# A recurrence whose second head pair has its tokens on the other half of the partitions

## The reference

```python
def step(state, inp):
    r_t, w_t, k_t, v_t, kk_t, a_t = inp
    sa = jnp.einsum('bhvk,bhk->bhv', state, -kk_t)
    state = (state * w_t[:, :, None, :]
             + sa[..., None] * (kk_t * a_t)[:, :, None, :]
             + v_t[..., None] * k_t[:, :, None, :])
    return state, jnp.einsum('bhvk,bhk->bhv', state, r_t)
_, y = lax.scan(step, s0, (r, decay, k, v, kk, a))       # 1040 tokens, 16 heads
# then, for each head: y minus its mean over the head's 64 channels, over its deviation,
# times ln_w plus ln_b, plus a bonus, times a gate
```

## Time and profile before

| | |
|---|---|
| median of three runs | 2782.72 us |
| the profiled execution | 2786.39 us |
| its span, first to last instruction | 2784.5 us |
| PE busy, share of the span | 2571.4 us, 92% |
| weight loads (PEld) busy | 2141.3 us, 77% |
| DVE, ACT, POOL busy | 1561.2, 1315.8, 316.7 us |
| mean granted clock of PE | 0.973 |
| stretch of the recurrence in it | 1211 to 1767 us |

### The profile page before, as it was taken

The page is one execution under the profiler, slowest core; times in us unless marked ns, Lnnn a source line. Parts: engine busy times, 40 slices in busy tenths (PEclk is TensorE's granted clock), DMA queues, the critical chain, the costliest instruction groups (busy, mean ns, idle before and its releaser), DMA issues. The chain is left out here.

```text
span 2784.5 us, 65171 instructions
## 1 busy us (share of the span) xinstructions
PE 2571.4 (92%) x27593; PEld 2141.3 (77%) x27593; DVE 1561.2 (56%) x2370; ACT 1315.8 (47%) x2266; POOL 316.7 (11%) x367
## 2 busy tenths in 40 slices
PE   6999999999989999989999999899895999999992
PEld 6989896777766766679999889778784888888882
DVE  4566664443035555544444444553326888888884
ACT  5655542222134444334444444462223777777771
POOL 0121222332000000001212222100001000000002
PEclk9999999999999999999999999999996999999996
DMA  4443342222122323212222201244355999999976
GB/s 110 156 164 137 131 148 72 92 92 74 40 94 66 101 63 130 86 46 80 55 61 58 58 21 33 77 114 136 118 187 212 392 392 396 398 391 393 398 298 257
DMA packets 162645, 440.46 MB, mean 158 GB/s; under 512 B 16295, under 2 KB 96825, under 8 KB 150097
## 3 DMA queue, kind: packets, MB, share of 16 engines
q1 hardware_dynamic: 146413, 381.95, 38.5%
q10 hardware_dynamic: 9060, 29.56, 2.8%
q0 software_dynamic: 6912, 25.17, 2.4%
HBM read 344.22 MB, written 92.41 MB: 157 GB/s over the span
## 5 line engine op out<-in xcount | busy, mean ns | idle before, releaser
L2610 DVE TENSOR_TENSOR ex_wL<-wx,ex_wH 128x2048 fp32r<-128x2048 f32 x192 | 436.0, 2285 | 46.6 <-ACT ex_wH L2514 44.8
L2514 ACT CAST ex_wH<-wx 128x2048 fp32r<-128x2048 f32 x192 | 366.4, 1911 | 94.3 <-PE ex_bank L2410 70.9
L2408 PE MATMUL ex_bank<-ex_wH,ex_xTH 128*128 128x512 f32 x512 | 200.5, 392 | 2.4 <-DVE ex_xTL L2615 2.4
L2409 PE MATMUL ex_bank<-ex_wH,ex_xTL 128*128 128x512 f32 x512 | 200.1, 391 | 0.0
L2410 PE MATMUL ex_bank<-ex_wL,ex_xTH 128*128 128x512 f32 x512 | 200.1, 391 | 0.0
L709 PE MATMUL ph_acc<-ph_wH,uH 128*104 128x512 f32 x480 | 192.5, 401 | 6.5 <-DVE ph_wL L721 6.5
L709 PE MATMUL ph_acc<-ph_wH,uL 128*104 128x512 f32 x480 | 189.5, 395 | 0.0
L709 PE MATMUL ph_acc<-ph_wL,uH 128*104 128x512 f32 x480 | 189.4, 395 | 0.0
L413 PE MATMUL pf_acc<-uH,pf_wH 128*128 128x348 f32 x648 | 160.3, 356 | 6.4 <-DVE pf_wL L533 6.4
L413 PE MATMUL pf_acc<-uL,pf_wH 128*128 128x348 f32 x648 | 138.6, 322 | 0.0
L413 PE MATMUL pf_acc<-uH,pf_wL 128*128 128x348 f32 x648 | 138.3, 322 | 0.0
(11 more groups left out here) (397 smaller groups left out, 6782.0 us busy)
## 6 DMA issues: line engine op xcount, KB each, us to landing
wx<-in_expert_w_gate SPq DMA_DIRECT2D x32, 2048.0 KB
wx<-in_expert_w_up SPq DMA_DIRECT2D x32, 2048.0 KB
wx<-in_expert_w_down SPq DMA_DIRECT2D x32, 2048.0 KB
s_y<-ex_y ACTq DMA_DIRECT2D x32, 512.0 KB, 10.1
fw<-in_w_in SPq DMA_DIRECT2D x27, 512.0 KB
hw<-in_w_in SPq DMA_DIRECT2D x6, 2048.0 KB, 10.1
s_qkT<-ph_stg ACTq DMA_DIRECT2D x4, 2080.0 KB, 6.9
mb_gt<-s_pT SPq DMA_DIRECT2D x16, 512.0 KB, 3.5
```

What stands on the lines that cost most here:

```text
L2408: nc.tensor.matmul(out, aH, bH, start=first, stop=False)
L2409: nc.tensor.matmul(out, aL, bH, start=False, stop=False)
L2514: nc.scalar.copy(wH[:, w, part], raw(j, s)[:, part]).then_inc(w_high, 1)
L2610: nc.vector.tensor_tensor(wL[:, w, part], raw(j, s)[:, part], wH[:, w, part], ALU.subtract).then_inc(w_low, 1)
```

## The change

The token side of the second pair (e = 1) changes halves: its head h has its tokens on the other half (`across`, `row`). Channel-token products (`m`, the raw matrix, `tok`, products with the state, the state's renewal) of the four heads then stand in four different quarters. Token-token products still stand in two. Two products that write the same partitions from different rows must not share a bank, so the pairs get banks of their own: 0 and 1 for `m`, the raw matrix `n` (before: step 2), `tok`, the output's part from the old state `h` and the transposes, one after another with a wait for the reader of the one before (`after_reading`), and 6 and 7 for q1 and the state.

Since an accumulation can't run over both sides of that split, sums move to DVE and ACT: q1 has the old state's part alone, the other part is made in q2 of the chunk before and copied by ACT with q2's result (`RA`, 256 columns), and DVE joins them to `R`. q4 and q5 become one piece, eight pieces a round instead of ten. The output's part from the old state is `h`, copied by ACT to `H`, and DVE adds it to the output as it writes `Y`. The `ln` rows are loaded by 32 small transfers where there were 8. The number of products stays: 17223 matmuls in the recurrence, before and after; PE's list there gets 156 instructions longer, all of them waits (35015 before and 35171 after, in the built programs, a float32 product counted as four).

```diff
-                for d in range(NF // 2):
-                    sp.dma_start(rows_[NF * j + 2 * d:NF * j + 2 * d + 2, :].rearrange("h (e p) -> h e p", e=2), ...
+                    for e, h in ((0, 0), (0, 1), (1, 0), (1, 1)):
+                        at = NF * j + 2 * d + across(e, h)
+                        sp.dma_start(rows_[at:at + 1, RD * e:RD * e + RD], heads[e, h:h + 1]).then_inc(consts, 16)
...
+def across(e, h):
+
+    return h if e == 0 else 1 - h
...
+        row = lambda e, h: here(across(e, h))
...
+            return (tokens(A) + first(6) + late(10) + piece() + old_state(A - 2)
+                    + first(7) + raw(B) + late(11) + piece()
+                    + first(8) + late(12) + piece()
+                    + ahead(A + 2) + first(9) + piece()
+                    + tokens(B) + second(6) + first(10) + piece() + old_state(B - 2)
+                    + second(7) + raw(A + 2) + first(11) + piece()
+                    + second(8) + first(12) + piece()
+                    + ahead(B + 2) + second(9) + piece())
...
+            def after_reading(*then):
+                for x in last_read:
+                    pe.wait_ge(*x)
+                last_read[:] = [then]
...
+                    for e, h in PAIRS:
+                        last = mm(bank[row(e, h), e, 2 * j * TC:(2 * j + 2) * TC].rearrange("p (a t) -> p a t", a=2),
                                   BK[z][half(h), e, j, cols], KR[z][half(h), e, :, cols], start=True, stop=True)
...
+                    else:
+                        pe.wait_ge(y_done, ch + OPEN)
+                        pe.wait_ge(seq_dve, added(ch - 1))
+                        for e, h in PAIRS:
+                            last = mm(bank[row(e, h), 6 + e, 384:384 + RD], KR[z][half(h), e, 0, cols], S[half(h), t % 2, e, :], start=True, stop=True)
...
+            def old_state(ch):
+                d, z, cols = place(ch)
+                after_reading(h_read, carried(ch))
+                for e, h in PAIRS:
+                    last = mm(bank[row(e, h), e, 0:RD], KR[z][half(h), e, 1, cols], S[half(h), ch % NCH % 2, e, :], start=True, stop=True)
+                last.then_inc(h_done, 1)
... (ACT)
+                    nc.scalar.copy(RA[0:PX, 0:n], bank[0:PX, 6, 128:128 + 128 * n].rearrange("p (k e d) -> p k e d", k=n, e=2)).then_inc(seq_act, 1)
+            def old_state(ch):
+                act.wait_ge(h_done, carried(ch))
+                act.wait_ge(y_done, ch + OPEN)
+                nc.scalar.copy(Hs[0:PX], bank[0:PX, 0:2, 0:RD]).then_inc(h_read, 1)
... (DVE)
+                        nc.vector.scalar_tensor_tensor(out=R[0:PX], in0=bank[0:PX, 6:8, 384:384 + RD], scalar=-1.0, in1=RA[0:PX, 1],
+                                                       op0=ALU.mult, op1=ALU.subtract).then_inc(rest_done, 1)
...
+                        tt(Y[x][0:PX, at:at + 2, :], out(2), Hs[0:PX], ALU.add).then_inc(y_done, 1)
```

More of the change, by code:

```diff
@@ L1281, in round_ @@
             A, B = 2 * r, 2 * r + 1
-            pieces = iter([(2 * r - 2 + j, q) for j in range(2) for q in (1, 2, 3, 4, 5)])
+            pieces = iter([(2 * r - 2 + j, q) for j in range(2) for q in (1, 2, 3, 4)])
             first = lambda n: [("solve", A, n)] if new else []
@@ L1300, in rwkv @@
+        SLOTS_ = 8
+        SPREAD = {"sum0": 0, "sum1": 1, "mean": 2, "sub": 2, "sq": 4, "var0": 9, "var1": 10, "std": 12, "rin": 13, "nrm": 13,
+                  "t0": 17, "e0": 17, "t1": 21, "e1": 21, "t2": 25, "e2": 25, "add": 26, "gate": 26}
         FIRST = [(NCH * (gi // 2) + GRP[gi % 2][1] - 1) // 2 + 2 for gi in range(2 * ND - 1)]
-        ORDER = [("m", 0, 0), ("m", 0, 1), ("m", 1, 0), ("m", 1, 1)]
+        ORDER = [("m", 0), ("m", 1), ("n", 0)]
         for r in range(NR + 1):
-            side = [(at - 10 * (r - FIRST[gi]), gi, name) for gi in range(2 * ND - 1) for name, at in SPREAD.items()
-                    if at // 10 == r - FIRST[gi]]
+            side = [(at - SLOTS_ * (r - FIRST[gi]), gi, name) for gi in range(2 * ND - 1) for name, at in SPREAD.items()
+                    if at // SLOTS_ == r - FIRST[gi]]
@@ L1390, in solve @@
                         pe.wait_ge(*at_dve(ch - 2, 12))
-                    for e, h in PAIRS:
-                        last = mm(at(bx, 0, e, h), KR[z][half(h), e, 0, cols], BK[z][half(h), e, 0, cols], start=True, stop=True)
-                elif n == 6:
-                    pe.wait_ge(*at_dve(ch, 2))
+                    pe.wait_ge(n_read, ch + 1 + OPEN)
                     pe.wait_ge(m_read, ch + 1 + OPEN)
@@ L1450, in tokens @@
                         src = V[z][half(h), e, cols] if j == 2 else BK[z][half(h), e, j, cols]
-                        last = mm(bank[here(h), 7, (2 * j + e) * RD:(2 * j + e + 1) * RD], src, c.ident[half(h), half(h)], start=True, stop=True)
+                        last = mm(bank[row(e, h), e, j * RD:(j + 1) * RD], src, c.ident[half(h), half(h)], start=True, stop=True)
                 last.then_inc(tok_done, 1)
-                last_read[:] = [(tok_read, ch + 1 + OPEN)]
             def seq(ch, q):
@@ L1499, in seq @@
-                last.then_inc(seq_pe, 1)
+                            mm(o(2, e, h), M4[row(e, h), m, e, 3, :], vv(e, h), start=True, stop=False)
+                        for h in range(2):
+                            last = mm(o(2, e, h), M4[row(e, h), m, e, 1, :], Uu[row(e, h), e, :], start=False, stop=True)
+                last.then_inc(seq_pe, 1)
+            def old_state(ch):
+                d, z, cols = place(ch)
+                after_reading(h_read, carried(ch))
+                for e, h in PAIRS:
+                    last = mm(bank[row(e, h), e, 0:RD], KR[z][half(h), e, 1, cols], S[half(h), ch % NCH % 2, e, :], start=True, stop=True)
+                last.then_inc(h_done, 1)
@@ L1506, in norm @@
                     pe.wait_ge(*gn_at(gi, "nrm"))
-                for x in last_read:
-                    pe.wait_ge(*x)
-                last_read[:] = [gn_at(gi, f"e{j}")]
+                after_reading(*gn_at(gi, f"e{j}"))
                 for t in range(4 * j, min(4 * j + 4, GN_SIZE[gi % 2] // 2)):
-                    last = tr(bank[:, 7, t % 4 * PX:(t % 4 + 1) * PX], Yq[0:PX, 2 * t:2 * t + 2, :].rearrange("p e d -> p (e d)"),
+                    last = tr(bank[:, 0, t % 4 * PX:(t % 4 + 1) * PX], Yq[0:PX, 2 * t:2 * t + 2, :].rearrange("p e d -> p (e d)"),
                               c.ident[0:PX, 0:PX])
                 last.then_inc(gn["pe"], 1)
-            walk({"m": masked, "solve": solve, "tok": tokens, "seq": seq, "gn": norm})
+            walk({"m": masked, "n": raw, "solve": solve, "tok": tokens, "seq": seq, "h": old_state, "gn": norm})
         @block.scalar
@@ L1586, in _ @@
             act.wait_ge(made, 1 + OPEN)
-            walk({"solve": solve, "tok": tokens, "seq": seq, "gn": norm})
+            walk({"solve": solve, "tok": tokens, "seq": seq, "h": old_state, "gn": norm})
         @block.gpsimd
@@ L1681, in seq @@
                         last.then_inc(seq_dve, 1)
+                    x = group(t)
+                    at = 2 * (t - GRP[x][0])
+                    if at == 0 and d > 0:
+                        dve.wait_ge(*gn_at(2 * d - 2 + x, "nrm"))
+                    if t == 0:
+                        nc.vector.tensor_copy(Y[x][0:PX, at:at + 2, :], out(2)).then_inc(y_done, 1)
+                    else:
+                        dve.wait_ge(h_read, carried(ch))
+                        tt(Y[x][0:PX, at:at + 2, :], out(2), Hs[0:PX], ALU.add).then_inc(y_done, 1)
             def norm(gi, name):
@@ L1707, in _ @@
             dve.wait_ge(made, 1 + OPEN)
-            walk({"m": masked, "solve": solve, "seq": seq, "gn": norm})
+            walk({"m": masked, "n": raw, "solve": solve, "seq": seq, "gn": norm})
 NG, EG = 4, 8
```

213 lines of the change are left out of this document (100 added, 113 removed).

## The result

The changed kernel takes 2791.86 us (median of 7 runs, 2790.43 to 2799.07), the kernel before on the same chip 2785.37 us (7 runs, 2782.28 to 2787.9). The ratio is 1.0030, 95% interval [1.0019, 1.0040]: slower by 0.3%. The forecast was 2781 and "no change". The profiled execution took 2790.65 us, its span is 2788.9. Executions of one kernel differ: the kernel before took 2777.8 to 2790.6 us on the five chips used, so small differences are read from medians and ratios, and one trace beside another says little under some 4 us.

What follows compares the result with a forecast made beforehand. The prediction took delivery of PE's instructions, about 3.92 us a packet, to bound the recurrence. Its terms, 0 - 3.2 + 0 + 2.4 - 1 + 0 = -1.8 us, took the median from 2782.7 to 2781; range 2750 to 2807.

Steps and rivals of the forecast that it cites:

- term 4: PE's instruction list in the recurrence: 156 more instructions are 0.6 of a packet, +2.4 us.
- The three stretches of the earlier trace: Recurrence stretches without transposes, whose instruction packets came 3.92, 3.93 and 3.88 us apart, read as one pace.
- Term 1: Channel-token products in four quarters: work per chunk falls, but instruction supply sets the interval, gain 0; at most 101 us.
- theory D: From the experiments: PE's next packet is requested after a first part of the present one; then a fixed way of 2.5 us.
- Term 2: Packet intervals with transposes, where PE's work exceeds supply: up to 6.4 us could go, half taken, -3.2.
- Term 3: New waits for results in each chunk, 0.76 us, lie in time PE would pause anyway: 0; uncovered 61 us.
- Term 5: First and last rounds of the recurrence, slower than the supply: less work counts, -1 us; ends -3 and +2.
- Term 6: 24 more small transfers at the kernel's start: hidden, 0; at worst +3 us.
- The toll: Rival: each packet's pause adds about 0.5 us to PE's work; 3.67 us a packet, -41 us, 2742; chance 0.15.
- Uncovered waits for `H`: Rival: the raw matrix's wait for the copy of `H` is half exposed in 77 chunks, +25 us, 2807; chance 0.15.
- Quarters that don't overlap: Rival: channel-token products don't run four deep; a chunk is 6.70 us, +8 to +16, about 2795; chance 0.13.

Runs made afterwards that it cites:

- n1: The changed kernel without three already fulfilled waits before q2's products, 158 instructions less: 2783.9 us, 1.0007 against the kernel before.
- k1: g1 with four instructions that only wait added in the first half of each packet of 256 instructions: 2822.1 us.
- k2: g1 with four instructions that only wait added in the second half of each packet of 256 instructions: 2783.1 us.
- e1: The changed kernel with `across` undone, so channel-token products stand in two quarters again; order, banks, sums and waits kept: 2797.9 us.
- n3: g1 with `across` undone, so channel-token products stand in two quarters: 2780.0 us.
- h2: g1 with ACT copying `H` before it makes the two decayed states SP: 2774.8 us.
- n2: The kernel before with the changed kernel's 32 small transfers for `ln` instead of 8: 2785.0 us in one run.
- g2: The kernel before without PE's repeated waits in the recurrence, 160 instructions less: 2778.0 us.
- e4: The kernel before with two of step 7's three products merged into one, 320 products less: 2797.2 us.
- e3: The changed kernel with two of step 7's three products merged into one, 320 products less: 2785.8 us.
- g1: The changed kernel without PE's repeated waits in the recurrence, 314 instructions less: 2771.8 us.
- e2: The changed kernel with 64 more long-fulfilled waits per chunk on PE, 2560 instructions more: 2896.3 us.
- j1: The changed kernel with each product of `tok` issued twice, 3840 instructions more: 2843.8 us.
- f3: The changed kernel with `tok` over both halves, no repeated waits, 82 further waits left out, `H` copied before SP: 2751.1 us.

## Why the prediction was wrong, point by point

**The step that failed is term 4**: "156 more instructions are 0.6 of a packet: +2.4 us, since the supply is the bound. This is the one sure term." All 156 only wait, and such an instruction is not 1/256 of a packet. n1 leaves out 158 waits and gets 8 us back (by the ratios 6.4), 51 or 41 ns each and not 16; with that the changed kernel and the one before can't be told apart. Behind it is what I made of the earlier trace rows: "one value, 3.92", a rate of delivery that knows nothing of what is in the packet. k1 and k2 show that it is no rate: four waits more in each packet's first half cost 90 ns each, in its second half 20. By the reading that fits them, a packet in which PE pauses takes the time that PE needs for a first part of it, until the next is asked for, and then a fixed way, 2.5 us from the transfer's start. What lies in the first part is paid in full, waits above all, and what lies in the second is covered. The three stretches of the earlier trace rows would agree with each other because the same mixture stands in all three; and counts of 26, 14 and 16 packets, each uncertain by one, could not have told rates from 3.8 to 4.1 us apart. The Trainium skill, "Runtime: NRT & Kernel Launch", section "Instruction fetch mechanics", calls crossing a boundary mostly hidden; here it was not: in 92% of the changed kernel's packets the first matmul behind the boundary starts more than 0.15 us after the one before it.

**Term 1, the quarters, gain 0.** The direction of the argument held: of 101 us at most 5 to 11 came (e1, n3). 0 was too little, probably for the same reason: shorter products in the first part bring the next packet forward. That is argued from theory D; only the size, within the range forecast for n3, speaks for it. The transposes' term is inside this figure.

**Term 2, transposes, -3.2.** Intervals with transposes fell by 0.40 us, in 16 to 18 places some 7 us: the whole of what I had halved. Half of it is the quarters' (in e1 such intervals take 4.26 us on average), the rest came with the new order, probably with the spreading of the groups of transposes.

**Term 3, new waits for results, covered, 0.** Right for `H`, the largest of them, as far as h2 tells. Its size was far off: 0.66 us a chunk were summed, and PE waited 4.5 us of 400 for `H`, 0.08 us a chunk:

```profile
PE rw_bank L1403 <- ACT rw_H L1584: 4.5, 14, 1.7
```

and h2, which takes most of that away, gains nothing. Here a wait for another engine's result was cheap, and a wait for what was long there dear.

**Term 5, begin and end, -1.** Wrong in sign. The last round's chain is longer: PE waits for DVE's `Y`, which now joins `H`, before q1. After, then before (start, length, idle before):

```profile
1769.80 0.33 PE L1490 MATMUL rw_bank<-rw_S,rw_kr 64*52 64x64 f32 x8 [0.78 <-DVE rw_Y L1725]
```
```profile
1762.25 0.32 PE L1468 MATMUL rw_bank<-rw_tok,rw_M 52*52 52x64 f32 x4 [0.41 <-ACT rw_Y L1560]
```

From step 9 of chunk 79 to the end it is 10.1 us where it was 8.3: +1.9 (8.3 to 9.0 in n2, g2 and e4, and 9.5 to 11.0 in e1, e3, g1, h2, n1 and n3, so the sign is sure). The beginning, to step 9 of chunk 3, lost 0.4, within what executions differ by.

**Term 6, the start's transfers, 0.** Nothing in n2 speaks against it, and a single run can't show more.

**The rivals.** The toll is excluded: it asked for 3.67 us a packet. Uncovered waits for `H` are excluded by h2, with the reservation made there. Quarters that don't overlap are excluded by the starts of L1512 and L1395. No rival had the cause, and the chance of 0.27 for "slower" sat on mechanisms that did not occur.

The account, from before to changed, +6.5 us by the medians and +8 by the ratios: 156 waits +6 to +8 (n1), quarters and transposes -5 to -11 (e1, n3), the gather behind the recurrence -2. So order, sums and the longer chain must be +5 to +15 by difference, a wide figure that adds up the noise of three comparisons. Measured beside each other without repeated waits (n3 and g2) they are +2 to +3, or +4 to +5 with the gather's 2 us taken off. Of this the +1.9 at the end can be seen; the rest was not taken apart. The prediction had no term for it beyond terms 3 and 5.

## What to carry to other kernels

Where pauses by "issue" return every 256 instructions of an engine, count its instructions by kind, and ask for each wait whether an earlier one already implies it: leaving out 314 of 35171 made this kernel 0.7% faster, more than four quarters instead of two did for a third of the recurrence's products. A pace read from pauses is the pace of that mixture of instructions, not a constant; before it prices an edit, a run with a handful of instructions added at a known place should confirm it. And compare a change with its bookkeeping taken out, too: here what the quarters gave was hidden by the waits that came with them.

## What the runs showed of the hardware that was not expected

- A fulfilled wait as an instruction of its own in PE's list cost 31 to 64 ns on average (e2, g1, g2, n1), 90 in the first half of a packet and 20 in the second (k1, k2). An instruction of a product cost 13.5 (j1). In the packed traces nearly every record of such a wait in the steady part lasts 51 ns, whatever it costs.
- With the changed order PE's clock stays low for longer at the recurrence's start. Windows from 1218 us, after and before; the clock stands in front of the last two numbers, and 0.50 is the lower of the two levels, 1.2 GHz:

```profile
1218.00:1221.00 3.00, 2.28 (x52) 1.97 (x50) 0.58 (x2) 1.14 (x3) 0.00 (x0) 0.50 0.00 0
1221.00:1224.00 3.00, 2.63 (x68) 2.40 (x68) 1.03 (x4) 0.25 (x1) 0.40 (x1) 0.50 0.03 5
1224.00:1227.00 3.00, 3.00 (x78) 2.92 (x73) 0.73 (x3) 1.39 (x4) 0.00 (x0) 0.50 0.00 0
1227.00:1230.00 3.00, 2.59 (x74) 2.46 (x74) 1.63 (x6) 0.24 (x1) 0.33 (x1) 0.66 0.02 5
```
```profile
1218.00:1221.00 3.00, 2.44 (x83) 2.16 (x81) 1.57 (x5) 0.58 (x2) 0.40 (x1) 1.00 0.00 0
```

  Before, the full clock came at about 1218, after at about 1229, 11 us later; from 1212 to 1221 PE was busy for 5.5 of 9 us, where it was 7.7 before. The traces of all runs agree: from the recurrence's first product to the full clock it is 6 to 8 us in the kernel before, `e4`, `g2` and `n2`, and 13 to 17 in the changed kernel and all that are built on it, e1 and n3 with their two quarters too (14.2 and 13.0). So it is not the four quarters that delay it. What it costs is small: step 9 of chunk 1, at 1229, is 3.6 us late, 1.9 more than the recurrence's first product, and that of chunk 3 is 2.1 late.
- `tok` over both halves (128 rows, 128 columns) took 66 ns a matmul, against 16 for 64 rows and 64 columns in four quarters: fewer instructions, but twice the time on PE (f3).
